# Where attention is normalised: scaling the output of each head, or its probabilities

## The reference, cut to what matters

```
s = q_h @ k.T * ATTN_SCALE            # [512, 512], masked by the index stage
p = softmax(s, axis=-1)               # rows: exp(s - peak) / total
o_h = p @ v                           # [512, 128]
y_h = o_h * silu(z_h)                 # z_h: the head's part of the gate
```

## Time and profile before

| | before |
|---|---|
| median of 3 runs | 1746.0 us (1745.29 to 1747.73) |
| the profiled execution, its time | 1746.0 us |
| its span, first to last instruction | 1744.3 us |
| mean granted clock of PE | 0.927 of full speed |
| busy: PE / DVE / ACT / POOL | 92% / 39% / 30% / 34% of the span |
| the loop over heads | from about 772 us to 946 us of the span |

### The profile page before, as it was taken

The page is one execution under the profiler, slowest core; times in us unless marked ns, Lnnn a source line. Parts: engine busy times, 40 slices in busy tenths (PEclk is TensorE's granted clock), DMA queues, the critical chain, the costliest instruction groups (busy, mean ns, idle before and its releaser), DMA issues. The chain is left out here.

```text
span 1744.3 us, 23553 instructions
## 1 busy us (share of the span) xinstructions
PE 1607.5 (92%) x9985; PEld 1359.6 (78%) x9985; DVE 688.3 (39%) x1383; ACT 519.1 (30%) x841; POOL 589.6 (34%) x247
## 2 busy tenths in 40 slices
PE   6998999999989988999998999999999767959899
PEld 6896885998978854878877998897887642649789
DVE  4031440331162545885544143312401555676331
ACT  2344224332222222234433122433221235212211
POOL 5323320343432274445542432242442350500213
PEclk9999999999999998999999999999999787569869
DMA  4223220225213221230113312442331000000102
GB/s 149 81 65 97 73 70 4 73 97 182 81 65 97 86 84 37 73 97 25 49 49 113 116 66 75 141 99 78 97 97 48 1 1 1 0 31 1 64 30 95
DMA packets 116723, 121.61 MB, mean 70 GB/s; under 512 B 14608, under 2 KB 110842, under 8 KB 116363
## 3 DMA queue, kind: packets, MB, share of 16 engines
q1 hardware_dynamic: 113072, 114.16, 20.7%
q10 hardware_dynamic: 3546, 5.94, 0.9%
HBM read 113.80 MB, written 6.29 MB: 69 GB/s over the span
## 5 line engine op out<-in xcount | busy, mean ns | idle before, releaser
L175 POOL TENSOR_TENSOR w_low<-w_ring,w_high 128x2048 fp32r<-128x2048 f32 (+2 forms) x95 | 421.4, 4437 | 901.6 <-ACT w_high L166 901.6
L191 PE MATMUL ps<-w_high,xT_high 128*128 128x256 f32 (+1 forms) x1056 | 306.7, 290 | 10.3 <-issue 6.9
L191 PE MATMUL ps<-w_low,xT_high 128*128 128x256 f32 (+1 forms) x1056 | 302.0, 286 | 0.0
L191 PE MATMUL ps<-w_high,xT_low 128*128 128x256 f32 (+1 forms) x1056 | 302.0, 286 | 0.0
L166 ACT ACTIVATE w_high<-w_ring 128x2048 fp32r<-128x2048 f32 (+2 forms) x95 | 174.1, 1834 | 364.6 <-PE ps L191 351.9
L191 PE MATMUL ps<-xT_high,w_high 128*128 128x512 f32 (+3 forms) x624 | 253.5, 406 | 8.7 <-DVE mix_a L724 7.7
L191 PE MATMUL ps<-xT_low,w_high 128*128 128x512 f32 (+3 forms) x624 | 249.2, 399 | 0.0
L191 PE MATMUL ps<-xT_high,w_low 128*128 128x512 f32 (+3 forms) x624 | 247.9, 397 | 0.0
L191 PEld LDWEIGHTS ps<-w_high,xT_high 128*128 128x128 f32 x1056 | 205.7, 195 | 16.1 <-issue 15.8
L191 PEld LDWEIGHTS ps<-w_low,xT_high 128*128 128x128 f32 x1056 | 205.8, 195 | 1.3 <-issue 1.2
L191 PEld LDWEIGHTS ps<-w_high,xT_low 128*128 128x128 f32 x1056 | 205.5, 195 | 0.0
(11 more groups left out here) (502 smaller groups left out, 2402.3 us busy)
## 6 DMA issues: line engine op xcount, KB each, us to landing
w_ring<-in_gla_w_in_dram SPq DMA_DIRECT2D x24, 1024.0 KB, 5.3
w_ring<-in_dsa_w_in_dram SPq DMA_DIRECT2D x19, 1024.0 KB, 5.1
w_ring<-in_w_in_dram SPq DMA_DIRECT2D x18, 1024.0 KB, 5.1
w_ring<-in_gla_w_out_dram SPq DMA_DIRECT2D x8, 1024.0 KB, 5.0
w_ring<-in_ple_gate_w_dram SPq DMA_DIRECT2D x8, 1024.0 KB, 5.1
w_ring<-in_dsa_w_out_dram SPq DMA_DIRECT2D x8, 1024.0 KB, 5.2
w_ring<-in_w_out_dram SPq DMA_DIRECT2D x8, 640.0 KB, 4.2
x_scratch<-x SPq DMA_DIRECT2D x4, 1024.0 KB, 6.6
```

The lines of the kernel that those rows point to most:

```text
L175: self.nc.gpsimd.tensor_tensor(self.w_low[:, i % RING, 0:k, 0:cols], self.w_ring[:, n % RING, 0:k, 0:cols], self.w_high[:, i % RING, 0:k, ...
L191: return self.nc.tensor.matmul(out, lhs, rhs, start=first, stop=last, skip_group_check=not check)
```

## The change

The division by the totals moves from the output to the probabilities.

- `inverse` and `scale_out` go. In their place DVE runs `normalise`: for each of the four tiles a reciprocal of one total per partition, then four multiplications in place, SBUF to SBUF, of 128, 256, 384 and 512 columns of fp32 by that value. For head h + 2 this stands in iteration h after `mask(h + 2)`, the shuffle and the gate's activation. Before the loop the order becomes mask(0), normalise(0), mask(1), normalise(1).
- PE's transposes of the probabilities wait for `prob_ready` (the multiplications) in place of `exps`.
- The product with v swaps its operands: v is stationary, the turned probabilities move, four matmuls of 512, 384, 256 and 128 columns. The output is feature-major at once, and `turn_out` goes (four transposes per head).
- The multiplication with the gate of head h moves to the end of DVE's iteration h, behind the product of head h, and ahead of the copies of head h + 1.

```diff
-                def turn_out(h):
-                    pe.wait_ge(sem["o_scaled"], past["o_scaled"] + h + 1)
-                    for j in range(NT):
-                        ins = nc.tensor.transpose(ps[:, 4 + h % 2, j * P:(j + 1) * P], o_tok[:, j, :], g.ident[:])
-                    ins.then_inc(sem["o_turned"], add("o_turned", 1))
...
-                    for j in range(NT):
-                        for i in range(j + 1):
-                            ins = g.product(ps[:, 4 + h % 2, j * P:(j + 1) * P], probT[:, i, j * P:(j + 1) * P], v[:, i, :], i == 0, i == j)
+                    for i in range(NT):
+                        ins = g.product(ps[:, 4 + h % 2, i * P:T], v[:, i, :], probT[:, i, i * P:T], i == 0, i == NT - 1, check=False)
                     ins.then_inc(sem["o_head"], add("o_head", 1))
-                turn_out(DSA_HEADS - 1)
...
+                def normalise(h):
+                    for j in range(NT):
+                        m = NT * h + j
+                        i = m % (2 * NT)
+                        dve.wait_ge(sem["exps"], past["exps"] + m + 1)
+                        nc.vector.reciprocal(inv[:, i:i + 1], total[:, i:i + 1]).then_inc(sem["inv_total"], add("inv_total", 1))
+                    for j in range(NT):
+                        m = NT * h + j
+                        i = m % (2 * NT)
+                        dve.wait_ge(sem["inv_total"], past["inv_total"] + m + 1)
+                        row = prob[:, h % 2, j, 0:(j + 1) * P]
+                        nc.vector.tensor_scalar(row, row, inv[:, i:i + 1], None, ALU.mult).then_inc(sem["prob_ready"], add("prob_ready", 1))
+
+                for h in range(2):
+                    mask(h)
+                    normalise(h)
                 for h in range(DSA_HEADS):
-                    inverse(h)
-                    copy_turned(h, 1)
-                    if h:
-                        gate_out(h - 1)
-                    copy_turned(h, 3)
+                    for j in range(1, NT, 2):
+                        m = NT * h + j
+                        dve.wait_ge(sem["prob_turned"], past["prob_turned"] + m + 1)
...
                     if h + 2 < DSA_HEADS:
                         mask(h + 2)
                     if n_scores + h < DSA_HEADS:
                         swap_query(n_scores + h)
                     if n_early + h < n_tiles:
                         project(n_early + h)
-                    scale_out(h)
-                gate_out(DSA_HEADS - 1)
+                    if h + 2 < DSA_HEADS:
+                        normalise(h + 2)
+                    dve.wait_ge(sem["o_head"], past["o_head"] + h + 1)
+                    if h >= 2:
+                        dve.wait_ge(sem["head_low"], past["head_low"] + h - 1)
+                    nc.vector.scalar_tensor_tensor(out=gated[:, h % 2, :], in0=ps[:, 4 + h % 2, :], scalar=1.0 if h < n_silu else 0.5, in1=zT[:, h, :],
+                                                                       op0=ALU.mult, op1=ALU.mult).then_inc(sem["head_done"], add("head_done", 1))
```

More of the change, by code:

```diff
@@ L1314, in _ @@
                 for h in range(DSA_HEADS):
[L1315 to L1318, removed]
-                    if h:
[L1320 to L1324, removed]
+                    for j in range(NT):
+                        m = NT * h + j
+                        pe.wait_ge(sem["prob_ready"], past["prob_ready"] + m + 1)
+                        if m >= 2:
+                            b = m - 2
+                            done = "probT_by_dve" if b % 2 else "probT_by_act"
+                            pe.wait_ge(sem[done], past[done] + b // 2 + 1)
+                        for i in range(j + 1):
+                            ins = nc.tensor.transpose(ps[:, 2 + m % 2, i * P:(i + 1) * P], prob[:, h % 2, j, i * P:(i + 1) * P], g.ident[:])
+                        ins.then_inc(sem["prob_turned"], add("prob_turned", 1))
+                        if n_early + h < n_tiles and j % 2:
+                            project(n_early + h, range(j // 2 * KD // 2, (j // 2 + 1) * KD // 2))
                     if h + 2 < DSA_HEADS:
@@ L1506, in mask @@
                         nc.vector.tensor_scalar(shift[:, i:i + 1], peak[:, i:i + 1], -ATTN_SCALE, None, ALU.mult).then_inc(sem["peak_shift"], add("peak_shift", 1))
[L1508 to L1532, removed]
@@ L1534, in _ @@
-                mask(0)
-                mask(1)
-                for h in range(DSA_HEADS):
-                    inverse(h)
-                    copy_turned(h, 1)
-                    if h:
-                        gate_out(h - 1)
-                    copy_turned(h, 3)
+                def normalise(h):
[4 more added lines that the diff above has]
+                        nc.vector.reciprocal(inv[:, i:i + 1], total[:, i:i + 1]).then_inc(sem["inv_total"], add("inv_total", 1))
+                    for j in range(NT):
+                        m = NT * h + j
[3 more added lines that the diff above has]
+                        nc.vector.tensor_scalar(row, row, inv[:, i:i + 1], None, ALU.mult).then_inc(sem["prob_ready"], add("prob_ready", 1))
@@ new lines, in _ @@
+                for h in range(2):
+                    mask(h)
+                    normalise(h)
+                for h in range(DSA_HEADS):
+                    for j in range(1, NT, 2):
+                        m = NT * h + j
+                        dve.wait_ge(sem["prob_turned"], past["prob_turned"] + m + 1)
+                        if h:
+                            dve.wait_ge(sem["o_head"], past["o_head"] + h)
+                        nc.vector.tensor_copy(probT[:, 0:j + 1, j * P:(j + 1) * P],
+                                                                     ps[:, 2 + m % 2, 0:(j + 1) * P].rearrange("p (i t) -> p i t", t=P)).then_inc(sem["probT_by_dve"], add("probT_by_dve", 1))
```

11 lines of the change are left out of this document (removed).

## The result

The changed kernel takes 1771.5 us (median of 4 runs, 1766.2 to 1775.2) against 1746.8 for the kernel before beside it: a ratio of 1.0132, 95% interval 1.0104 to 1.0160. It is slower by some 24.7 us; 57 were forecast. The direction was right, the time lies in the range, and the size is less than half of the forecast.

What follows compares the result with a forecast made beforehand. PE, busy 92% of the span, was taken as the bound, with any DVE hold beyond 0.2 us a head paid by PE in full. Forecast: 1746.0 + 46.2 (late DVE, net of savings) + 10.5 (clock) = 1803 us, range 1760 to 1816.

Steps and rivals of the forecast that it cites:

- PE's saving: Per head on PE: 0.43 us from dropping turn_out and 0.06 from the product with v in 8 records.
- The date: DVE's copy of transpose tile 1 must end by L + 8.0 (L: PE starts the scores); 0.2 us of room.
- The odd heads: Heads 1 to 11: low part before third multiplication, weight split before fourth; 5.1 us late, +4.6 a head, +27.6 together.
- the first rival: Odd heads: POOL's low part asks after the third multiplication starts, so only it delays the fourth; 1765 us, chance 0.18.
- Heads 0, 2, 4, 6: POOL's low part (not in head 0) and rotation steps go between DVE's multiplications: +1.5 in head 0, +7.2 in the others.
- the 13.5 us case: Heads 2, 4, 6: the first multiplication precedes POOL's low part, the copy ends at L + 10.2, the head takes 13.5.
- the 14.8 one: Heads 2, 4, 6: POOL's low part precedes the first multiplication, the copy ends at L + 11.5, the head takes 14.8.
- The start: Before the loop normalise(0) waits for exponentials and a weight split, delaying mask(1) and PE's scores by 5.4; +6.3 us in all.
- Heads 8 and 10, and the end: Heads 8 and 10, without rotation or split: -0.5 together; heads 12 to 15, first two bound by DVE's chain: +4.1.
- The clock: PE at half clock after seven waits of about 5 us (six odd heads, the start), 1.5 each: +10.5; bounds 0 and 21.
- rival 4: The clock stays low: as forecast, with 3 us for each wait and 1 to 2 in even heads; 1816 us, chance 0.12.
- the sum of 46.2: All forecast changes in us, clock excluded: 27.6 + 7.2 + 1.5 - 0.5 + 6.3 + 4.1.

Runs made afterwards that it cites:

- one, two and three small operations: Changed kernel with one, two or three 128x1 DVE operations, results unused, ahead of normalise in odd heads: 1767.1, 1773.3 and 1786.0 us.
- short rotation: Changed kernel with POOL's three rotation steps in the loop working on 8 of 512 columns: 1759.9 us, ratio 1.0083 to the kernel before.
- Masks first: Changed kernel with mask(0), mask(1) ahead of normalise(0), normalise(1) before the loop: 1761.1 us, ratio 1.0096 to the kernel before.
- the form with sums: Changed kernel with each multiplication also writing its row's sum to a tile nothing reads: 1753.1 us, ratio 1.0043 to the kernel before.

## Why the prediction was wrong in size

**PE's saving: right.** 0.49 us a head was forecast; without the division a head is 11.25, 0.51 less. The product saves 0.08 (forecast 0.06).

**The date: right.** DVE's copy of tile 1 had to be done by L + 8.0, and "all the room is used up, and anything that holds DVE for longer than 0.2 us is paid by PE in full". In the odd heads the copy ends at L + 8.1 (809.68 + 0.41) and the head is 0.27 longer than unheld. In head 2 it ends at L + 10.2 (823.28 + 0.41, with L = 813.50), 2.2 past the date, and PE waits 2.17. One premise was wrong and cost nothing: not every wide DVE operation of the loop before has an operand in PSUM. The shuffle has none, but in heads 6 and 7 it ran while POOL was idle.

**The odd heads: the step that failed.** "The third multiplication goes between the two POOL operations, to 7.2; the split, to 11.55; the fourth, to 12.0", +27.6 us in six heads. They measured -1.2 in five, and +2.3 in head 11, for another reason. What was off is small. The forecast placed the third multiplication at about L + 5.7 (5.0, then 0.29 and 0.35 with 0.05 between), 0.3 behind the low part. I had these durations from multiplications that stand alone: in the attention of the earlier trace rows a reciprocal comes between any two. Back to back each starts 0.08 us before the end of the one in front, and the four take 1.26 in place of 1.7 (at 783.04 in the changed kernel). That, and a start at L + 4.90 in place of 5.0, puts the third at L + 5.34, ahead of the low part, whose date L + 5.43 was right to 0.01.

This has the outcome of the first rival, "three get through", but not its reason. There POOL was to ask later than its date, 0.35 us behind its semaphore, and "some 0.1 us" was the distance from the 0.24 of a row to that. In fact POOL came on its date and DVE was 0.4 us earlier than I had it. That the measured margin is 0.09 us as well is chance. The rival gave +0.2 to +0.4 a head against before, with the copy done at L + 8.7; measured are -0.2 and L + 8.1, since that copy too was made of the long durations. The runs with one, two and three small operations show that the mechanism stood: a tipped head takes 17.2 to 17.4 us, some 1.5 of it clock, where the forecast has 16.35 and 1.5 of clock beside it; PE waits 4.54 of the 5.1 forecast.

**Heads 0, 2, 4, 6: right.** Forecast +1.5 and +7.2; measured +1.3 and, with 1.6 us of half clock in each of heads 2 and 6, +8.6, or 5.5 without it. The first multiplication is ahead of the low part by 0.07 us: the 13.5 us case, 13.58 in head 4, and never the 14.8 one. The short rotation takes it away.

**The start: right.** Forecast +6.3 and 1.5 of clock; measured +7.3 from the first scores to those of head 0, 2.9 of it clock. As forecast, normalise(0) waits for the exponentials and then for the split, for the split 0.7 us, and mask(1) comes behind it. Masks first takes 5.4 of the 7.3 away.

**Heads 8 and 10, and the end.** -1.0 (forecast -0.5); heads 12 to 15 +3.9 (forecast +4.1), and head 11 +2.3, which is the same chain of DVE one head earlier than I had put it. That 3.9 is so near to 4.1 is luck: the forecast holds 2.2 us for a copy behind the split of head 11, where the fourth multiplication lasted 1.49 and stood ahead of the split, and no clock; the 6.2 us from head 11 on hold 3 to 4.3 of clock.

**The clock: right in total, by luck.** Seven waits of 5 us at 1.5 each were forecast, 10.5 us, and the loop lost 9 to 10.4. But there was only one such wait, before the loop, and it cost 2.9. The rest are five waits of 2.0 to 2.2 us with 3.4 us at half clock each, at 1.4 to 1.6 us: the price that I had put on a wait of 5, on waits that only rival 4 had priced, and only in the even heads. Which waits of 2 us go with half clock stays open (in heads 2 and 6 but not 4, and with the masks first in 6 alone of the three). Without the clock the time would be near 1762, at the lower end of the range.

Together the loop gives -1.2 + 2.3 + 1.3 + 8.6 - 1.0 + 7.3 + 3.9 = 21.2 us, and the two traces 194.26 - 173.01 = 21.25. Take 9 to 10.4 of clock from it, and 11 to 12 us stand against the sum of 46.2. Of the 34 to 35 between them, 24.2 are the five odd heads (forecast +23.0, measured -1.2) and 5.5 to 7 are head 11 and what follows (forecast 4.6 + 4.1, measured 2 to 3); the start and heads 2, 4 and 6 are near 2 each. The 3.5 us between the loop's 21.2 and the 24.7 of the medians lie outside the loop, where two profiles of this very kernel differ by 8; what decides how long the clock is at half there was not found.

## What to carry to other kernels

When two engines exclude each other, the price is set by who asks first, and the list of starts has to be made from durations of back-to-back operations in the same form, not from operations that stand apart. If two starts come out within a few tenths of a us of each other, treat both orders as cases of equal weight; better, take the operation off the contested interface (a form that writes a sum, or another engine with room), since 0.18 us more on DVE in four heads turned a margin that held into a loss of 20 us. A saving on the bound engine is kept where the added work fits the room that its engine has at that very moment of the head: ACT had it in every head, DVE in the form with sums in heads 0 to 10 and no longer in those behind. And price short waits of PE too: here half clock, most of it beside waits of 2 us, made up nearly half of the loop's loss.

## What the runs showed of the hardware

- Four multiplications in place, SBUF to SBUF, by a value per partition overlap in their records by 0.08 us: 0.26, 0.34, 0.41 and about 0.5 us take 1.26 together.
- The point at which POOL's waiting operation gets in first was sharp: with 0.41 to 0.42 us between the starts one of four heads tipped, with 0.47 none, with 0.35 to 0.36 all.
- The form with a sum per row took 0.73 us for 512 columns in place of 0.5, and POOL's operations did not lengthen it.
- With waits of 2.15 us in heads 2, 4 and 6 went 3.4 us at 1.2 GHz in heads 2 and 6 and none in head 4, with waits of 2.0 to 2.1 in heads 11, 12 and 13 3.4 us each, with the wait of 4.35 us before the loop 6.8 us; waits of 1.5 and 1.6 us left the clock at full. A stretch of 3.4 us cost 1.4 to 1.6 us, that of 6.8 cost 2.9.
- The form with a sum was not held, yet took as long before the loop (1.93 us for four) as the plain one with its hold (1.94): equal waits of PE didn't mean that nothing was held.
- Outside the loop the same kernel's two profiles differ by 8 us, at a mean granted clock of 0.913 and 0.919 and with 22 us more at half clock in the slower one.
